# Merge and retention turned to channel-major products in a two-layer transformer kernel

## The reference

```
h = rms_norm(x);  proj = h @ w_in                      # 1024 x 10240
out_a = stick_breaking_attention(...) * silu(sb_g)     # 8 heads of 128
qb, kb = rotary(r_q), rotary(r_k) / 16                 # retention: 4 heads, 256 wide
ret   = chunkwise_retention(qb, kb, r_v)
out_b = rms_norm(ret) * silu(r_g)
p_a, p_b = out_a @ w_branch_sb, out_b @ w_branch_ret
merged = sigmoid(m_sb + b_merge[0]) * p_a + sigmoid(m_ret + b_merge[1]) * p_b
x = x + merged @ w_out
```

## Time and profile before

| | us |
|---|---|
| median of 3 runs (2349.3 to 2351.01) | 2350.4 |
| the profiled execution | 2359.4 |
| its span | 2357.6 |
| busy: PE / PEld / DVE / ACT / POOL | 2245.7 / 1835.1 / 1075.3 / 957.2 / 365.1 |
| mean granted clock of TensorE, share of full | 0.961 |

### The profile page before, as it was taken

The page is one execution under the profiler, slowest core; times in us unless marked ns, Lnnn a source line. Parts: engine busy times, 40 slices in busy tenths (PEclk is TensorE's granted clock), DMA queues, the critical chain, the costliest instruction groups (busy, mean ns, idle before and its releaser), DMA issues.

```text
span 2357.6 us, 29446 instructions
## 1 busy us (share of the span) xinstructions
PE 2245.7 (95%) x11727; PEld 1835.1 (78%) x11727; DVE 1075.3 (46%) x2018; ACT 957.2 (41%) x1761; POOL 365.1 (15%) x602
## 2 busy tenths in 40 slices
PE   7999998899997899999999999998999999999998
PEld 6778776667797788888887788886888888788776
DVE  4344444443346443566556655544523434424431
ACT  4464544343455243456455645642222323223210
POOL 3200112542602120000000000004300212010011
PEclk9999898889589899999999999999999999999999
DMA  5521344443742341111111202112221112343222
GB/s 159 193 82 61 93 115 150 105 124 90 241 186 89 116 131 50 36 54 58 45 49 41 68 27 63 31 41 63 76 72 45 50 50 85 106 148 122 81 94 85
DMA packets 171609, 210.82 MB, mean 89 GB/s; under 512 B 36560, under 2 KB 124720, under 8 KB 169936
## 3 DMA queue, kind: packets, MB, share of 16 engines
q1 hardware_dynamic: 150752, 141.51, 19.3%
q0 software_dynamic: 20720, 67.43, 8.9%
HBM read 151.45 MB, written 53.77 MB: 87 GB/s over the span
## 4 chain that ended last, share of the span: by engine, by line
PE 86%; DVE 4%; ACT 4%; POOL 2%; DMA 2%; issue 1%; SPq 0%; POOLq 0%; DVEq 0%; ACTq 0%
PE PS L1629 19%; PE PS L1631 19%; PE PS L1630 19%; PE PS L1597 6%; PE PS L1907 3%; PE PS L1886 3%; PE PS L1623 2%; PE PS L1624 2%; PE PS L1625 2%; PE PS L1690 2%; PE PS L1716 2%; PE PS L1943 1%; PE PS L1956 1%; ACT TM L1965 1%; PE PS L1747 1%
## 5 line engine op out<-in xcount | busy, mean ns | idle before, releaser
L1629 PE MATMUL PS<-WH,HH 128*128 128x512 f32 x2112 | 866.7, 410 | 16.7 <-DVE WK L2353 10.5
L1631 PE MATMUL PS<-WH,HL 128*128 128x512 f32 x2112 | 831.3, 394 | 0.0
L1630 PE MATMUL PS<-WH,HH 128*128 128x512 f32 x2112 | 829.9, 393 | 0.0
L1629 PEld LDWEIGHTS PS<-WH,HH 128*128 128x128 f32 x2112 | 401.0, 190 | 102.3 <-DVE WK L2353 12.1
L1631 PEld LDWEIGHTS PS<-WH,HL 128*128 128x128 f32 x2112 | 400.3, 190 | 87.5
L1630 PEld LDWEIGHTS PS<-WH,HH 128*128 128x128 f32 x2112 | 401.8, 190 | 72.3
L1965 ACT ACTIVATE TM<-PS 128x512 f32<-128x512 f32 (+3 forms) x285 | 154.2, 556 | 327.5 <-PE PS L1631 257.3
L2325 DVE SCALAR_TENSOR_TENSOR WH<-RAW,WK,WH 128x512 fp32r<-128x512 f32 (+2 forms) x248 | 179.9, 747 | 230.8 <-ACT WH L1965 229.7
L1965 ACT ACTIVATE WH<-RAW,WK 128x512 fp32r<-128x512 f32 (+2 forms) x248 | 170.3, 705 | 83.7 <-PE PS L1631 39.9
L1597 PE MATMUL PS<-WK,TM 128*128 128x128 f32 x776 | 117.0, 280 | 38.8 <-DVE TM L2330 10.5
L1597 PEld LDWEIGHTS PS<-WK,TM 128*128 128x128 f32 x776 | 95.1, 143 | 65.0 <-issue 11.7
(11 more groups left out here) (306 smaller groups left out, 2834.3 us busy)
## 6 DMA issues: line engine op xcount, KB each, us to landing
RAW<-in_w_in SPq DMA_DIRECT2D x200, 256.0 KB, 3.0
RAW<-in_w_out SPq DMA_DIRECT2D x32, 256.0 KB, 3.3
sig_d<-WK POOLq DMA_DIRECT2D x32, 256.0 KB, 2.4
WK<-sig_d POOLq DMA_DIRECT2D x32, 256.0 KB, 3.4
WK<-in_rpb POOLq DMA_DIRECT2D x16, 480.0 KB, 4.7
RAW<-in_w_in SPq DMA_DIRECT2D x32, 192.0 KB, 3.1
dnc_d<-TM SPq DMA_DIRECT2D x12, 512.0 KB, 3.5
TM<-dnc_d SPq DMA_DIRECT2D x10, 512.0 KB, 4.9
```

The lines of the kernel that those rows point to most:

```text
L1629: e.matmul(ps, hh, wt[:, 0:width], start=k == 0, stop=False)
L1630: e.matmul(ps, hh, wt[:, 512:512 + width], start=False, stop=False)
L1631: mm = e.matmul(ps, hl, wt[:, 0:width], start=False, stop=k == 7)
```

## The change

`tiles_of` gives pairs for all m, q, sb and rt blocks, so that these 12 blocks are computed by channels. The gates' bias becomes one number per lane, transferred once. The products of q and k come out with channels on the partitions, in the form that the scores and the output need; only k is turned, from channels to tokens, 4 batches a head, with its decay folded into ACT's copy; `rk` is gone. The rotation works on 128 channels by 256 tokens. `ret_side` starts ahead of the q block and takes each rotation when its tiles are out; the turns and the first scores start when the first tokens are rotated instead of behind the last. The merged rows come out with channels on the partitions: the turn `mg` is gone, and item `mc` copies and subtracts them from SBUF. The turns `oa` and `ob` wait until four tiles of the block are done (a half of the tokens).

```diff
 def tiles_of(b):
+    if BLOCKS[b][0] in "mq" or 31 <= b < 35:
+        return [(c, th) for th in range(2) for c in range(4)]
     return list(range(8))
...
-        "rk": [("dve", 1300)],
+        "mc": [act(512), dve(512)],
...
     def ret_side(h):
...
+        else:
+            yield has("rr", h - 1, 7)
+        plan.spawn(ret_turn(h))
         plan.spawn(ret_inner(h))
+        for n in range(8):
+            yield has("ev", BLOCK[f"q{h}"], (n // 2 % 2 * 2 + 1, n // 4))
+            put("rr", h, n)
+            yield
...
+    def ret_turn(h):
+        for j in range(4):
+            yield has(*turned(h, 2 * j))
+            put("rt", h, j)
+            yield
...
         for t in range(8):
-            yield lambda: len(left) > t
+            yield lambda: len(left) >= t // 4 * 4 + 4
+            st(stage, t)
...
+    def merge_in():
+        for th in range(2):
+            for k in range(8):
+                yield has("ed", BLOCK["rt1"], (3, th))
+                put("mc", th, k)
+                yield
...
                 elif kind == "rt":
                     h, j = a
...
+                    for said in ("o", "po"):
+                        w.wait_ge(*at[(*keys_turned(h, 2 * j), said)])
+                    if j or h:
+                        w.wait_ge(*at["rt", h if j else h - 1, (j - 1) % 4, "out"])
                     for i in range(4):
-                        mm = tr(bank(4, 128, i * 128), tokens(bx)[:, j % 2 * 4 + i, o:o + 128])
+                        mm = tr(bank(4, 128, i * 128), chunk(channels_of(h)[:, 2 + i % 2, :], 2 * j + i // 2))
...
+                elif kind == "mc":
+                    th, k = a
+                    w.wait_ge(*at["g", BLOCK["rt1"], (3, th), 7, "done"])
+                    w.wait_ge(*at["ed", BLOCK["rt1" if k >= 4 else "rt0"], (k % 4, th), "out"])
+                    copy(HHb[:, k, th * 512:(th + 1) * 512], merged(k, th)).then_inc(*w.sig(*item, "hi"))
...
-                        tt(sgb[i], ps, tail, ALU.add).then_inc(*w.sig(*item, "out"))
+                        j = int(name[1]) * 8 + int(name[2]) * 4 + t[0]
+                        ts(sgb[i], ps, br[:, j:j + 1], None, ALU.add).then_inc(*w.sig(*item, "out"))
...
-                    dma(CS, cossin.rearrange("s (t p) c -> p s t c", p=128), c_rt)
+                    dma(CS, cossin.rearrange("s p t -> p s t"), c_rt)
...
-                    dma(by_tile(ob_d, h * 256, 256), tokens(ret_bufs(h)[0])[:, :, 0:256], c_ob)
+                    for dh in range(2):
+                        dma(by_tile(ob_d, h * 256 + dh * 128, 128),
+                            channels_of(h)[:, dh, :].rearrange("p (t k) -> p t k", t=8), c_ob)
```

More of the change, by code:

```diff
@@ L899, in sb_front, with turned @@
             yield
+    def turned(h, c):
+        return "rr", h, c // 4 * 4 + 2 + c // 2 % 2
     def ret_side(h):
@@ L907, in ret_side @@
             put("rc")
-        for t in range(8):
-            put("rr", h, t)
-            yield
[L911 to L917, removed]
+        else:
+            yield has("rr", h - 1, 7)
+        plan.spawn(ret_turn(h))
+        plan.spawn(ret_inner(h))
+        for n in range(8):
+            yield has("ev", BLOCK[f"q{h}"], (n // 2 % 2 * 2 + 1, n // 4))
+            put("rr", h, n)
+            yield
         yield has("vz", h)
@@ L941, in ret_state @@
     def ret_state(h):
+        if h:
+            yield has("ro", h - 1, 7)
         for c in range(7):
+            yield has("rt", h, c // 2)
             if c:
@@ L972, in schedule @@
         if name[0] == "m":
-            put("br", name)
+            if name == "m00":
+                put("br")
             if name == "m11":
@@ L1000, in feeds @@
     def feeds(b):
+        tiles = tiles_of(b)
         def ready(t):
-            for n in (0, 1) if t == 0 else (t + 1,):
+            i = tiles.index(t)
+            for n in (0, 1) if i == 0 else (i + 1,):
                 if n < 8:
                     put("fd", b, n)
-            plan.drain(has("st", stage_of(b), t, 1))
+            plan.drain(has("mc", t // 4, 7) if b >= 35 else has("st", stage_of(b), t[1] * 4 + 3, 1))
         return ready
     for b in range(31, 37):
-        second = b in (32, 34)
-        if second:
+        if b == 32:
             left.clear()
-            plan.spawn(swap("ob" if b == 32 else "mg"))
-        gemm(b, feeds(b), left.append if second else None)
+            plan.spawn(swap("ob"))
+        if b == 34:
+            plan.spawn(merge_in())
+        gemm(b, feeds(b), left.append if b == 32 else None)
     put("end")
@@ L1094, in build @@
         GTs = tail[0:64, 384:512]
+        br = tail[:, 0:16]
         DNFIX = WKW - 512 - 1008
@@ L1216, in xin, with merged @@
             return TM[:, 1 + t // 4, (t % 4) * 1024:(t % 4 + 1) * 1024]
-        def merged(t):
-            return TM[:, 1 + t // 4, (t % 4) * 1024:(t % 4 + 1) * 1024]
+        def merged(k, th):
+            o = k % 4 * 1024 + th * 512
+            return TM[:, 1 + k // 4, o:o + 512]
         def tokens(buf):
@@ L1925, in _ @@
                     h, c = a
-                    w.wait_ge(*at["rt", h, 7, "out"])
+                    for said in ("o", "po"):
+                        w.wait_ge(*at[(*keys_turned(h, c), said)])
                     if c > 1 or h:
@@ L1942, in _ @@
                     for dh in range(2):
-                        mm = e.matmul(bank((7, 3)[c % 2], 256, dh * 256), tokens(bx)[:, c, 256 + dh * 128:384 + dh * 128],
+                        mm = e.matmul(bank((7, 3)[c % 2], 256, dh * 256), KT[h % 2][:, c, dh * 128:(dh + 1) * 128],
                                       tokens(by)[:, c, 0:256], start=True, stop=True)
@@ L2056, in _ @@
                             w.wait_ge(*at["rm", before, 1, "o"])
-                            w.wait_ge(c_ob, 16 * (before + 1))
-                        copy(tokens(buf_of(b))[:, t, :], ps).then_inc(*w.sig(*item, "out"))
+                            w.wait_ge(c_ob, 32 * (before + 1))
+                        if name[0] == "q":
+                            o = channels_of(int(name[1]))[:, t[0], t[1] * 512:(t[1] + 1) * 512]
+                        else:
+                            o = tokens(buf_of(b))[:, t, :]
+                        copy(o, ps).then_inc(*w.sig(*item, "out"))
                 elif kind == "nq":
@@ L2264, in _ @@
                     w.wait_ge(*at[(*item, "t")])
-                    copy(RQK[j // 4][:, j // 2 % 2, j % 2 * 512:(j % 2 + 1) * 512], bank(4)).then_inc(*w.sig(*item, "out"))
+                    w.wait_ge(c_rt, 48)
+                    copy(KT[h % 2][:, 2 * j:2 * j + 2, :], bank(4).rearrange("p (t c) -> p t c", t=2),
+                         rc[:, 4 + h:5 + h]).then_inc(*w.sig(*item, "out"))
                 elif kind == "ro":
@@ L2618, in _ @@
                 elif kind == "rr":
[L2619 to L2623 removed]
+                    h, n = a
+                    t1, t2, cols = rotated(h, n)
+                    c, s = CS[:, 0, cols], CS[:, 1, cols]
+                    w.wait_ge(*at["ev", BLOCK[f"q{h}"], (n // 2 % 2 * 2 + 1, n // 4), "out"])
                     w.wait_ge(c_rt, 48)
@@ L2836, in _ @@
                 elif kind == "br":
-                    g, cb = int(a[0][1]), int(a[0][2])
-                    before = {"m01": "m00", "m10": "m01", "m11": "m10"}.get(a[0])
-                    if before:
-                        w.wait_ge(*at["ed", BLOCK[before], 7, "out"])
-                    dma(tail, b_merge[g:g + 1, cb * 512:(cb + 1) * 512].to_broadcast([128, 512]), c_br)
+                    dma(br, b_merge, c_br)
                 elif kind == "sw":
```

140 lines of the change are left out of this document (69 added, 71 removed).

## The result

The changed kernel takes 2317.6 us (median of 4 runs, 2317.1 to 2318.9) against 2350.7 for the kernel before on the same chip (2349.3 to 2354.9). The ratio is 0.9857, 95% interval 0.9844 to 0.987: 33.1 us less, where 30.3 were predicted. The profiled execution took 2317.6 us, its span and 1.8 us around it. One execution of the repetition e9 took 12.4 ms; it is left out, and e9's median is that of the other four.

What follows compares the result with a forecast made beforehand. PE was taken as the bound, busy 2245.7 of 2357.6 us. Terms -15.5 - 7.4 - 8.4 + 1 = -30.3 us, summed on the profile and taken off the median 2350.4, gave 2320 us, range 2316 to 2325.

Steps and rivals of the forecast that it cites:

- Form of the product: In 12 blocks, 768 triples of matmuls swap standing and moving operands; claimed to cost 0, bounds -2 to +2 us.
- Merge's turn: In rt1, eight tiles each lose 1.94 us of transposes and waiting for DVE's addition, copies staying hidden: -15.5 us.
- Retention's turns: In retention, only k is turned, so 16 batches of four transposes go at 0.46 us each: -7.4 us.
- Turns in m11: Attention output's turns move behind retention's last output; 7.0 us of waits and 1.5 of low clock go: -8.4 us.
- Head 0's wait: PE's wait in q1 for retention's first rotations comes sooner but stays the same, 9.5 us against 9.64.
- lag: Behind head 0's wait, later rotations might come late for their turns in the q blocks: +1 us.
- rw: Its store, once a head, uses 512 B rows in two transfers, its reader two blocks away: 0.
- rival B: Retention's rotations late for half of the 16 turn batches, about 1 us each: 2328.6 us, chance 0.11.
- A: The waits in m11 come back elsewhere, at block borders or in head 3's chain: 2328.5 us, chance 0.11.
- D: DVE falls behind in the q blocks, each turn batch a whole rotation late: 2364 us, chance 0.03.
- E: Products by channels slower after all, or merged copies hold up o0: 2350 only if both, chance 0.03.
- C: More gain: tables 3 us earlier, no rotation lag (1), m11 at its bound (1.6 more): 2314.5 us, chance 0.10.

Runs made afterwards that it cites:

- e9: The changed kernel run once more, unaltered, beside other kernels on one chip: 2318.3 us, against 2355.8 for the kernel before there.
- e1: Kernel before with only the merge's half of the change, attention's turns later included, retention as before: 2326.3 us, 24.9 below before.
- e3: Kernel before, all by tokens, with only the turns of attention's output placed later, behind retention's last output: 2342.0 us, 9.2 below before.
- e4: Kernel before with only the turns of the merged rows placed one tile later, transposes kept: 2343.7 us, 7.5 below before.
- e8: Changed kernel with each copy and subtraction of the merged rows made twice: 2322.1 us, tail 731.6 us, no new wait of PE.
- e2: Kernel before with only retention's half (q blocks by channels, k alone turned), merge as before: 2343.4 us, 7.8 below before.
- e5: Changed kernel with each of retention's 16 batches of turns written twice, 64 transposes more: 2325.2 us, 7.6 over the changed kernel's first median.
- e7: Kernel before with its planner told that retention's tables take 10.5 us to land: 2337.8 us, 13.3 below before.
- e12: Kernel before, all by tokens, with attention's turns later, merged rows turned one tile later and planner told of the tables: 2326.7 us, 29.1 below before.
- e10: Changed kernel with its planner told that retention's tables take 10.5 us to land, second run: 2308.5 us, 0.980 of before.

## Why the prediction was right, step by step

- **Form of the product, 0.** Right: 390 ns a matmul, and e1 less e3 is 15.7 (medians) and 16.7 us (tails), where the turn alone explains 15.5. m00 and m01, ahead of the landmark, show nothing either.
- **Merge's turn, -15.5.** Right, and its split is now measured: 8.2 of waits (e4) and 7.3 of transposes. The copies' cover held with room for twice their work (e8).
- **Retention's turns, -7.4.** Right: e2 gave -7.8 in all, of which about 0.9 is a shorter wait of head 0 (8.7 against 9.6), and e5 gave +4.6 to +7.6 for putting as many transposes back.
- **Turns in m11, -8.4.** Right in size: e3 gave 9.2 and a tail of 8.3. The 7.0 of waits are firm. The 1.5 for the lower clock was read from one execution, and e4 and e7 show that it may be twice that or nothing.
- **Head 0's wait, the same, and a lag of +1.** The wait stayed (9.5 predicted, 9.1 to 9.5 measured). The lag is the one term that failed: none of the later turns waited for a rotation. The rotations took (1617.92 - 1596.60)/7 = 3.0 us each, not 2.8, and were still 1.4 us ahead of the third batch, so rival B was closer than its 0.11 may sound.
- **rw, 0.** Nothing in the traces speaks against it.
- **Profile against median.** I took the 9.0 us by which the profiled execution exceeded the median off as it stood. The landmark shows why this was right: the excess over the changed kernel was there at 949.5 us, ahead of every block that the change alters. That the execution shown was so high was chance; the prediction gave no reason for its step.

The sum less the lag is 31.3, the measured 33.1 (tail 32.7, and 31.9 with e9's). Of the 1.4 to 1.8 us left, 0.5 is head 0's wait, and the lower level lasted 2.7 us behind that wait in the changed kernel against 3.3 before and 4.2 in e9, so some of it is chance. The rest stays open. Of the rivals, A and B fell with e1 and e2, D needed 36 us of waits where there is only head 0's, E fell with e1 and e8, and C named 3 us for the tables and 1 for a lag: the lag it had right. What I had not asked is how much the places of the turns alone would do: 15.1 of the 32.7 us (e3 and e4), and with the planner told of the tables e12 gets 29.1 us by tokens.

## What to carry to other kernels

Price a removed instruction on the bounding engine by start-to-start spacing, and split a gain into instructions and waits before crediting it to the new layout: here 28.5 us of waits could be had by moving work in the queue alone (e12), and 15 us more by removing it (e10 against e12). Tell a planner that sets a fixed order what a transfer takes; an unpriced load of some 10 us left a wait of 9 us that two layouts shared. When single executions drift in a stretch that no edit touches, measure from a landmark behind it, and check which edits reach ahead of it.

## What the runs showed of the hardware that I had not expected

- The landmark came at 1594.1, 1594.1, 1584.2, 1583.9 and 1590.1 us in five kernels that are alike up to it (before, e3, e4, e7, e12), with a mean granted clock from 600 to 800 us of 0.78 to 0.85. Ten microseconds of a 2350 us program are chance here, more than several of the edits.
- A wait of PE of about 2 us is sometimes followed by the lower clock level and sometimes not, in the same order of instructions: one spell in the kernel before, two in e4, none in e7. The wait of some 9 us for head 0 brought it in all of before, changed and e1; removing it gained 10.7 to 11.7 us of tail (9.7 by medians on one chip) for 9.1 to 9.5 of wait.
- Transposes in a row cost 0.11 us each (0.43 for four), and leaving them for a 512-column product a tenth of a microsecond more once.
